# Expert layer of a diffusion step: one weight load behind a gather, the last weights behind the sums, one root for five tiles

## What is computed

```
def _ec_moe(h, w_router, w_gate, w_up, w_down):        # 16 experts, each picks its own tokens
    cap = EC_CAPACITY_FACTOR * T // N_EXPERTS            # 64 latent rows, 16 context rows
    probs = softmax(h @ w_router)
    gates, idx = top_k(swapaxes(probs, 1, 2), cap)
    xs = h[bidx, idx]
    a = silu(xs @ w_gate) * (xs @ w_up)
    y = (a @ w_down) * gates
    return zeros_like(h).at[bidx, idx].add(y)
...
x = x + gate2 * _ec_moe(h)
y_prompt, y_sample = _rmsnorm(xp, g_final), _rmsnorm(xs, g_final)
```

## Time and profile before

| | us |
|---|---|
| median of 3 runs | 854.32 (853.18 to 854.4) |
| the profiled execution's own time | 853.98 |
| its span, first to last instruction | 852.1 |
| TensorE busy in it | 830.2 (97%) |
| mean granted clock | 0.997 |

### The profile page before, as it was taken

One profiled execution on the slowest core, in us unless ns is written; L12 is line 12 of the kernel. 1 busy time (PEld: TensorE's weight loads), 2 busy tenths in 40 slices (PEclk: granted clock), 3 DMA queues, 4 the chain that ended last, 5 costly groups with the idle time before them and its releaser, 6 DMA issues.

```text
span 852.1 us, 14545 instructions
## 1 busy us (share of the span) xinstructions
PE 830.2 (97%) x6034; PEld 455.7 (53%) x6034; DVE 502.6 (59%) x1233; ACT 233.3 (27%) x462; POOL 60.6 (7%) x74
## 2 busy tenths in 40 slices
PE   6999999999999999999999999999999999999995
PEld 5798899899897876333333333333333333333322
DVE  3676552869366568876556456456456465465436
ACT  5557543544243334020110110111011011011015
POOL 1000000000000002011011011011011011010033
PEclk9999999999999999999999999999999999999998
DMA  9955625352418939999999999999999999999993
GB/s 329 303 203 190 224 82 198 113 197 75 136 34 343 367 131 326 425 409 428 415 407 430 410 410 429 411 413 423 415 411 419 419 412 417 424 409 412 427 349 147
DMA packets 51014, 275.28 MB, mean 323 GB/s; under 512 B 5210, under 2 KB 14526, under 8 KB 38788
## 3 DMA queue, kind: packets, MB, share of 16 engines
q1 hardware_dynamic: 45484, 255.68, 74.3%
q0 software_dynamic: 3936, 13.77, 5.5%
q10 hardware_dynamic: 1528, 4.90, 1.5%
HBM read 260.83 MB, written 13.57 MB: 322 GB/s over the span
## 4 chain that ended last, share of the span: by engine, by line
PE 89%; DMA 3%; DVE 3%; ACT 2%; SPq 1%; issue 1%; POOLq 0%; DVEq 0%
PE pair L2466 26%; PE pair L2069 17%; PE pair L2445 12%; PE pair L2491 12%; PE pair L2306 7%; PE pair L2500 6%; PE pair L2009 2%; PE pair L2104 2%; DMA scale_b<-in_w_mod 2%; DMA xs<-hn,gather_idx 1%; PE pair L2227 1%; PE pair L2217 1%; PE pair L2018 1%; DVE aT L1847 1%; DMA out<-x_sb 0%
## 5 line engine op out<-in xcount | busy, mean ns | idle before, releaser
L2466 PE MATMUL pair<-ring,xT 128*64 128x512 f32 x1024 | 223.9, 594 | 1.4 <-ACT xT L1126 1.4
L2466 PEld LDWEIGHTS pair<-ring,xT 128*64 128x64 f32 x1024 | 72.1, 137 | 143.9 <-issue 141.7
L2491 PE MATMUL pair<-ring,aT 128*64 128x512 f32 x512 | 113.4, 595 | 0.6 <-DVE aT L1847 0.6
L2445 PE MATMUL pair<-ring,xT 128*32 128x512 f32 x1024 | 113.4, 594 | 0.0
L1126 ACT ACTIVATE xT<-xT,mod,scale 128x64 f32<-128x64 f32 x120 | 41.4, 427 | 218.9 <-DVE xT L1847 218.9
L1847 DVE STREAM_TRANSPOSE xT<-xs 32x256 f32<-32x256 f32 x180 | 78.3, 435 | 4.4 <-DMA xs<-hn,gather_idx 1.4
L1847 DVE STREAM_TRANSPOSE aT<-act_l 32x128 f32<-32x128 f32 x256 | 77.5, 303 | 4.1
L2491 PEld LDWEIGHTS pair<-ring,aT 128*64 128x64 f32 x512 | 35.8, 137 | 76.8 <-issue 76.8
L2069 PE MATMUL pair<-hT_hi,w_hi 128*128 128x320 f32 x320 | 76.0, 319 | 0.0
L2445 PEld LDWEIGHTS pair<-ring,xT 128*32 128x32 f32 x1024 | 31.5, 110 | 79.4 <-issue 79.4
L2069 PE MATMUL pair<-hT_lo,w_hi 128*128 128x320 f32 x320 | 73.1, 310 | 0.0
(11 more groups left out here) (332 smaller groups left out, 940.6 us busy)
## 6 DMA issues: line engine op xcount, KB each, us to landing
ring<-in_w_up SPq DMA_DIRECT2D x32, 2048.0 KB, 29.0
ring<-in_w_down SPq DMA_DIRECT2D x32, 2048.0 KB, 19.7
ring<-in_w_gate SPq DMA_DIRECT2D x31, 2048.0 KB, 24.9
p1w<-in_w_mod SPq DMA_DIRECT2D x8, 2048.0 KB, 7.9
p1w<-in_w_in SPq DMA_DIRECT2D x5, 2048.0 KB, 7.9
p1w<-in_w_mod SPq DMA_DIRECT2D x7, 1024.0 KB, 11.8
x_sb<-in_x_sample SPq DMA_DIRECT2D x8, 512.0 KB, 5.8
p1w<-in_w_out SPq DMA_DIRECT2D x2, 2048.0 KB, 8.7
```

Source lines behind the costliest of these rows:

```text
L2445: ins = mm(ctx_ps[32 * g:32 * g + 32, :], xt[:, 4 * half + j, CAP_L:96], w[:, j, n * 512:(n + 1) * 512], start=half == 0 and j == 0, stop= ...
L2466: ins = mm(ps[64 * n:64 * n + 64, :], xt[:, kk, 0:CAP_L], w[:, j, n * 512:(n + 1) * 512], start=kk == 0, stop=kk == KC - 1)
L2491: ins = mm(y_ps[0][r:r + 64, :], aT[:, j, 64 * fh:64 * fh + 64], wd[:, j, n * 512:(n + 1) * 512], start=fh == 0 and j == 0, stop=fh == 1 a ...
```

## The change

1. SP issues load 9 (expert 1, up, second half) only when `gather(1)` has landed (`xs_full[1]`); all later loads stand behind it on SP.
2. VectorE, expert 0: the turns of expert 1's rows (`tokens`) come before `choice()`, which came first.
3. The very last load (95, down of expert 15, second half) is no longer issued when its place is free, but behind the five loads of the sums, in two halves of 1 MB. The second counts on another semaphore (that of ring place 0, once load 90 has landed), and TensorE waits for it before the ninth of the last 16 matmuls of L2491.
4. ScalarE, expert 15: the square of tile 0 comes before Silu of the latent rows, those of tiles 1 to 4 before Silu of the context rows; then the table load, and one root for all five tiles. VectorE takes one inverse, ahead of the turns `aTc`.
5. ScalarE scales tiles 0, 1, 3, 4 in a row, all before the square of expert 15's rows; `finish_fourth` is gone. The stores go 0, 1, 3, 2, then the context tile.

```diff
+LAST_GATE = 16 * (6 * (E - 1) // TURNS + 1)
@@ SP
             sp.wait_ge(sums_ctx, 32)
+            sp.wait_ge(xs_full[1], 16)
             load_rows(9)
...
-            for n in range(6 * (E - 1), 6 * E):
+            for n in range(6 * (E - 1), 6 * E - 1):
                 load_later(n)
+            def load_last_half(half, signal):
+                src = w_down[0, E - 1, 512:1024, :].rearrange("(p k) n -> p k n", p=P)
+                sp.dma_start(ring[(6 * E - 1) % TURNS][:, 2 * half:2 * half + 2, :], src[:, 2 * half:2 * half + 2, :]
+                             ).then_inc(signal, 16)
...
+            load_last_half(0, w_full[(6 * E - 1) % TURNS])
+            sp.wait_ge(w_full[6 * (E - 1) % TURNS], LAST_GATE)
+            load_last_half(1, w_full[6 * (E - 1) % TURNS])
-            for t, signal, value in ((2, fin_ready, 1), (0, fin_scaled, 1), (3, fin_ready, 2), (1, fin_scaled, 2)):
+            for t, signal, value in ((0, fin_scaled, 1), (1, fin_scaled, 2), (3, fin_scaled, 3), (2, fin_ready, 1)):
@@ ScalarE
-                act.wait_ge(finv_ready, 1 if t < 3 else 2)
+                act.wait_ge(finv_ready, 1)
...
+                if k == E - 1:
+                    final_squares(0, 1)
                 act.wait_ge(gul_done, e + 1)
                 a.activation(in_fours(act_l[:, :]), ...Silu)
                 if k == E - 1:
-                    final_squares(0, 1)
+                    final_squares(1, NT)
...
-                    final_squares(1, 3)
-                    final_root(0, 3)
-                    final_squares(3, NT)
-                    final_root(3, NT)
+                    final_root()
                     final_scaled(0, 0)
+                    final_scaled(1, 1)
+                    final_scaled(3, 2)
+                    final_scaled(4, 3)
                     last_square(0)
-                    final_scaled(1, 1)
                     last_sqrt(0)
-                    final_scaled(4, 3)
@@ VectorE
+                if k == E - 1:
+                    dve.wait_ge(froot_ready, 1)
+                    inverse_after(rms, slice(0, NT), rms[:, 0, 0:NT], finv_ready)
                 dve.wait_ge(act_c_ready, e + 1)
...
                 if k == 0:
+                    tokens(e + 1, k + 1)
                     choice()
                     dve.wait_ge(g2_ready, 2)
-                    tokens(e + 1, k + 1)
                 if k == E - 1:
-                    dve.wait_ge(froot_ready, 1)
-                    inverse_after(rms, slice(0, 3), rms[:, 0, 0:3], finv_ready)
                     finish_third()
...
-                    dve.wait_ge(froot_ready, 2)
-                    inverse_after(rms, slice(3, NT), rms[:, 0, 3:NT], finv_ready)
-                    finish_fourth()
@@ TensorE, down of the latent rows
                     for j in range(4):
+                        if k == E - 1 and (fh, j) == (1, 2):
+                            pe.wait_ge(w_full[6 * (E - 1) % TURNS], LAST_GATE + 16)
```

More of the change, by code:

```diff
@@ L619, in _ @@
                 sp.dma_start(x_sb[:, t, :], sum_l[tile(t), :] if t < NT - 1 else sum_c[0:P, :]).then_inc(sums_back[t], 16)
-            for t, signal, value in ((2, fin_ready, 1), (0, fin_scaled, 1), (3, fin_ready, 2), (1, fin_scaled, 2)):
+            load_last_half(0, w_full[(6 * E - 1) % TURNS])
+            sp.wait_ge(w_full[6 * (E - 1) % TURNS], LAST_GATE)
+            load_last_half(1, w_full[6 * (E - 1) % TURNS])
+            for t, signal, value in ((0, fin_scaled, 1), (1, fin_scaled, 2), (3, fin_scaled, 3), (2, fin_ready, 1)):
                 sp.wait_ge(signal, value)
                 sp.dma_start(y_sample[0, tile(t), :], x_sb[:, t, :]).then_inc(fin_out, 16)
-            sp.wait_ge(fin_scaled, 3)
+            sp.wait_ge(fin_scaled, 4)
             sp.dma_start(y_prompt[0], x_sb[:, 4, :]).then_inc(fin_out_c, 16)
@@ L728, in _, with times_gain @@
                 add_rows(e)
+            def times_gain(i, t):
+                pool.wait_ge(sums_back[t], 48 if t < NT - 1 else 32)
+                g.tensor_tensor(final_gain[:, i, :], x_sb[:, t, :], gfin[:, :], ALU.mult).then_inc(fin_pool, 1)
             pool.wait_ge(y_added, 16 * (E - 1))
@@ L735, in _ @@
             pool.wait_ge(gfin_in, 16)
-            for i, t in enumerate((0, 1, 3, 4)):
-                pool.wait_ge(sums_back[t], 48 if t < NT - 1 else 32)
-                g.tensor_tensor(final_gain[:, i, :], x_sb[:, t, :], gfin[:, :], ALU.mult).then_inc(fin_pool, 1)
+            for i, t in ((0, 0), (1, 1), (2, 3), (3, 4)):
+                times_gain(i, t)
             pool.wait_ge(fin_out, 64)
@@ L1128, in tokens, with final_root @@
                 ins.then_inc(xT_lat, 1)
-            def final_root(lo, hi):
-                act.wait_ge(fss_ready, hi)
-                a.activation(rms[:, 2, lo:hi], rms[:, 0, lo:hi], ACT.Sqrt, bias=eps_col[:, 0:1]).then_inc(froot_ready, 1)
+            def final_root():
+                act.wait_ge(fss_ready, NT)
+                a.activation(rms[:, 2, 0:NT], rms[:, 0, 0:NT], ACT.Sqrt, bias=eps_col[:, 0:1]).then_inc(froot_ready, 1)
             def final_scaled(t, i):
-                act.wait_ge(finv_ready, 1 if t < 3 else 2)
+                act.wait_ge(finv_ready, 1)
                 act.wait_ge(fin_pool, i + 1)
@@ L1938, in finish_third @@
             def finish_third():
+                dve.wait_ge(finv_ready, 1)
                 v.scalar_tensor_tensor(out=x_sb[:, 2, :], in0=x_sb[:, 2, :], scalar=rms[:, 5, 2:3], in1=gfin[:, :],
                                        op0=ALU.mult, op1=ALU.mult).then_inc(fin_ready, 1)
-            def finish_fourth():
-                dve.wait_ge(fin_pool, 3)
-                v.tensor_scalar(x_sb[:, 3, :], final_gain[:, 2, :], rms[:, 5, 3:4], None, ALU.mult).then_inc(fin_ready, 1)
             def spread(dst_l, dst_c, row):
```

## The result

| | before | after |
|---|---|---|
| median of 8 runs each, us | 854.04 | 857.27 (856.0 to 859.13) |
| ratio, 95% interval | | 1.0038 [1.0026, 1.0051] |
| profiled execution, own time and span | 853.98 and 852.1 | 857.96 and 856.1 |

The changed kernel is slower by 3.2 us. The forecast was 852.7, with a range up to 855.0: wrong in size and in sign.

A forecast was written before the change was run, and what follows sets the result against it. TensorE, busy 97% of the span, was taken as the bound. Stores -1.5 us and -0.1 left of the other terms made -1.6: 852.4 profiled, 852.7 as median against 854.32, range 851.2 to 855.0.

The forecast's parts named there:

- Term 1: Expert 1's start: with load 9 held back the gather lands in 3.5 us and TensorE starts 1.4 us earlier.
- costed at nothing: Expert 1: gather 2, issued some six us later, is turned by 387.1, before TensorE needs it at 387.5.
- Term 2: SP's load stream from load 9 on: starts 2.5 us late, cutting TensorE's lead at load 87 to 1.1 us.
- D: Delay of SP's load stream from holding load 9: 2.5 us, with bounds of 1.3 and 10.5.
- G: Landing time of the first gather: 353.3, with bounds of 352.5 and 361.4.
- Term 4: One root at expert 15: no wait at Silu, 0.5 us to spare; y_l starts at 838.3, against 838.45.
- Term 3: Last 2 MB: moving load 95 behind the sums gives them 5.3 us; a 0.6 us stall at its second half.
- the waits eat the stores' gain: Rival, chance 0.24: stream delay near 4 us, load 87 late by 0.4; gain only 0.1, time 854.2.
- No stall at Silu: Sign at expert 15: Silu does not wait for a square; if it does, the prediction is wrong.
- Term 5: Stores at the end: the chain ends in VectorE instead of a store, -1.5 us.
- The last 2 MB are late: Rival, chance 0.10: sums or halves late at load 95's ninth matmul or the root; slower, 856.0 at 3.3 us.
- The gather was slow by itself: Rival, chance 0.06: gather still lands at 361.4, TensorE stands 6.9 us at load 87; time 860.7.

The follow-up runs named there:

- order_only: The kernel before with only the turns of expert 1's rows moved ahead of choice(); 855.56 us, ratio 1.0022.
- undo_gate: The changed kernel without SP's wait for gather 1 before load 9; 853.22 us, ratio 0.9995 against the kernel before.
- gate_issue: The changed kernel, but SP holds load 9 only until gather 1 is issued, not landed; 853.91 us, ratio 1.0003 against the kernel before.
- before_last: The kernel before with only the last load moved behind the sums, in two halves; 853.46 us, ratio 0.9998.
- ungated_early: The changed kernel without load 9's wait and with gather 2 issued right behind gather 1; 852.84 us, ratio 0.9984 against the kernel before.
- half_ahead: The changed kernel with the first half of load 95 issued ahead of the sums, the second still behind; 857.68 us, ratio 1.0042 against the kernel before.
- root_stores: The kernel before with only the end's new order: squares ahead of each Silu, one root, one inverse, new store order; 855.36 us, ratio 1.0022.
- undo_last: The changed kernel with load 95 back whole in its old place ahead of the sums; 861.61 us, ratio 1.0086 against the kernel before.

## Why the prediction was wrong

**Term 1 held, where it was claimed.** TensorE starts expert 1 at the end of expert 0, 1.4 us earlier; the gather came down from 11.6 to 4.7 us (forecast 3.5). The cover of gather 2, "costed at nothing", failed by 0.52 us: it was issued at 365.67 and took 11.1 us as assumed, but the chain of turns, `act_l` and first turns was longer than the 0.4 us I left. The chain that I added up went from the turns straight to `act_l`; in the trace ScalarE scales expert 2's rows first (from 380.44, 2.76 us), Silu of expert 1 starts only at 383.11, and VectorE stands 0.84 us for it. In `order_only` it was 0.92, in `undo_gate` 1.30.

**Term 2 is the step that failed: D.** The formula was D = G + 1.0 - 350.5 - 1.3 = 2.5, with "about one us after G" for the restart. By what the queue moved, D is 5.0. Of the 2.5 us too little, 1.2 are the gather (4.7, not 3.5). The restart: nothing moves from 353.70 to about 354.5, then two us at 238 GB/s where the stream makes 431, which is 0.9 us of data short; 1.7 where I took 1.0, and 0.3 more for the 410 GB/s of the next six us. The queue was dry some 0.3 us earlier than I took it. Together that is the 2.5. The 6.3 us at load 9's own landing are more than the stream's delay: when it landed, SP's queue had moved 3.03 MB since the gather's issue, before 2.61, so more of the loads behind it had gone ahead of its last packets. I took the price of a restart as the first part of a small transfer. Nearer rows were there: in the kernel before, a 2 MB load of `p1w`, issued at 128.07 with the DMA engines idle, took 7.6 us, and load 9 took 8.6 here and 9.4 in `gate_issue`, against 4.9 us (2.1 MB at 431 GB/s) for one in the stream.

What follows from D is as the prediction had it: the stream never catches up. Load 87 had 3.6 us of margin and came 5.9 us later, so TensorE must come out 2.3 late; Silu of expert 14 is 2.48 late. In `gate_issue` load 87 came 3.0 us later, within the margin.

From there the loss goes through the sums. The prediction had the last of them at 830.2; it landed at 835.47, 836.22 on the clock of before, **6.0 us later than forecast**. `y_l` followed 8.2 us behind it (843.67), where the prediction's own chain had 8.1: that part of term 4 held. Of the 6.0 us, 2.5 are D, and 2.3 are term 3, below. With both sizes put right the sum gives 852.7 + 2.5 + 2.3 = 857.5, against 857.27 measured. That it comes so near is in part luck: 1.2 of the 6.0 us I can't assign, and the profiled execution from which they come (857.96) lies 0.7 above that median. The rival "the waits eat the stores' gain" stopped at D of 4; D at 5 lay between the bounds of 1.3 and 10.5, and no case of mine held it.

**Term 3 failed in its size.** "The bytes in all are the same" is true, but they can't move at the same time: the sums wait for the scatter-add, and while it runs almost nothing else is queued. `before_last` shows it without the gate. Its clock is 0.33 us ahead (gather issued at 349.42); on that of before, the sums are issued at 819.88 instead of 822.07 and the last landed at 829.83 instead of 832.83 (the 833.03 of the prediction is 0.2 too late). That is 3.0 us of gain, where I took 5.3. There the roots still have time; in the change they have none. Against `before_last`, and each from its gather's issue, the last of the sums lands 6.4 us later in the change: the scatter-add is issued 2.75 us later, takes 10.9 us instead of 8.3, and from the issue of the sums to the last landing it is 11.0 us instead of 9.95. The halves' stalls come to 1.57 + 0.45 us where 0.6 was forecast, but they stand beside this chain.

**Term 4.** "No stall at Silu" failed by 0.4 us (2.48 to 2.90 in the table), one of the signs that the prediction named for being wrong. The 0.5 us to spare hung on D; without the gate they are there, and `undo_gate` shows no wait. The root behind the last sums holds `y_l` up, as said above: VectorE starts it 1.26 us after TensorE's product is through, and TensorE then waits 0.52 us before its sum.

**Term 5 held in kind**: the last link before POOL's two scatters is VectorE and not a store (it is the last write of `y_l`, 848.82). The end of the span is 5.06 us behind `y_c` (forecast 5.0), and between `y_c` and the end the table gets back 6.16 - 4.75 = 1.4 us. `undo_gate` shows the gain undisturbed: its Silu of expert 15 is 0.53 us late and its end 0.80 us early (851.6 - 350.05 = 501.55 against 502.35), 1.3 us won behind Silu. In `ungated_early` the same stretch wins nothing, since TensorE waits 0.44 us for the second half and 0.52 for `left_l`: being 1.2 us earlier than `undo_gate` it meets the next limit.

**The rivals.** "The last 2 MB are late" (0.10) named two places. TensorE's waits for the halves were there, 1.57 + 0.45 us, but cost nothing: `half_ahead` takes them away and ends no earlier. The other, the root behind the fifth tile, is the place where the time was lost. That rival put it down to the sums and halves alone; here D stands behind it, for `undo_gate`, with the same root, is as fast as before. "The gather was slow by itself" is out: 4.7 us with the queue dry, and 10.6 to 11.6 behind running loads in all kernels without a gate but one.

## What to carry over

Here a wait that drained a saturated queue delayed it by more than the 4.7 us that the small transfer took: 5.0 us, though the small transfer's own bytes had been moved in between. Price the restart by a lone load of the same size (7.6 to 9.4 us here, against 4.9 in the stream), and compare the whole with the smallest margin of any later load. Measure the delay by the bytes that the queue has moved, not by one landing. A stream that never pauses keeps such a delay to its end, so a gain of 1.4 us at the front cost 4 us at the back. If a small transfer must go first, hold the queue only until that is issued: that cost 2.2 us of the stream here instead of 5.0. And before calling a wait of the busiest engine a cost, look whether it stands in the chain that ended last.

## What the hardware showed that I had not expected

- **A small gather behind 2 MB loads starts late rather than shares badly.** Packets of POOL's queue in the window of before from 4 to 6 us behind the gather's issue, 353.75 to 355.75:

```profile
q1 hardware_dynamic: 40, 0.44, 53.0%
q0 software_dynamic: 87, 0.36, 44.2%
```

  Once the gather's packets appear they get nearly half of the engines. The Trainium skill, page "DMA: Bandwidth & Descriptors", section "Queues, rings and completion order", has the queues served in turn, packet by packet; the near equal shares of time agree with turns, the counts of 40 and 87 packets don't agree with turns of one packet each. What the rule does not give is the start: nothing of the gather moves in the first four us with loads running, but from about 1.5 us on with the queue dry. After that comes a thin tail, 0.12 and 0.05 MB in the next two stretches of 2 us, that keeps the landing to 11.6 us. In `root_stores` the same gather took 6.1 us. It was issued 2.5 us later than before (352.24), while load 9 landed at much the same time (357.24, before 356.79), and SP issued the next load only at 354.71, before at 352.23. From 355 to 357 SP's queue moved 0.18 MB there and POOL's 0.50. So the gather met the queue nearly dry; that this is the reason was not tried by itself.
- **One transfer alone takes longer than its bytes and a fixed part.** The Trainium skill, page "DMA: Bandwidth & Descriptors", section "Anatomy of one DMA — SWDGE (gpsimd) path", fits 2.0 us plus the bytes at 436 GB/s for a DMA that POOL issues, which would be an estimate of 3.2 us for the gather. No run here came that low: 4.6 to 5.0 us where load 9 waited for its landing.
- **The last scatter-add took from 8.3 to 11.4 us** for the same rows: 8.3 in `before_last` and `undo_gate`, 10.2 before, 10.9 to 11.4 in the five kernels that wait for the landing of the gather, but 11.3 in `order_only` too, which has no gate. In the nine kernels that have not the whole of load 95 queued ahead of the sums it landed within 0.9 us of load 94 (824.40 and 824.57 in the change, 819.49 and 818.61 in `before_last`). That the stream beside it sets its time fits this, but was not tried by itself.
- **A pause of 2.1 us in TensorE was followed by a granted clock of 0.72**, a mean of the 2.4 GHz level and the 1.2 GHz level, over five us, in `root_stores`. In `undo_last`, 835 to 840, it was 0.50, the lower level, behind the pause of 6.07 us, and the 32 matmuls took 9.07 us. After the change's pauses of 1.50 and 1.57 us the clock stayed at 1.00, and so it did in `half_ahead` after a pause of 2.12 us at the same place, whose 32 matmuls took 7.09 us. So the length of the pause alone doesn't tell these cases apart.
